# Renumbering the features of the expert gate/up matmuls so that the bf16 parts of the residual are written contiguously

## The reference, cut to what matters

```python
h = h + mixer(rmsnorm(h, norm_mix[i]))
h = h + hier_moe(rmsnorm(h, norm_ffn[i]), ...)

# hier_moe
grp_logits = xt @ w_grp + b_grp                      # 4 groups
exp_logits = einsum("td,gde->tge", xt, w_rt) + b_rt  # 4 experts in each
gate = ...   # top group, in it top 2 experts, softmax weights; (T, 16)
h = silu(einsum("td,edf->tef", xt, w_gate)) * einsum("td,edf->tef", xt, w_up)
y = einsum("tef,efd->td", h * gate[:, :, None], w_down)
```

## Time and profile before

| | |
|---|---|
| median of 3 runs | 1512.72 us |
| span of the profiled execution, first to last instruction | 1510.4 us |
| what lies around the span (median less span) | 2.3 us |
| TensorE busy | 1399.9 us (93%) |
| VectorE busy | 550.6 us (36%) |
| ScalarE busy | 438.2 us (29%) |
| GpSimd busy | 54.7 us (4%) |
| DMA | 480.62 MB, mean 318 GB/s |

### The profile page before, as it was taken

One profiled execution on the slowest core, in us unless ns is written; L12 is line 12 of the kernel. 1 busy time (PEld: TensorE's weight loads), 2 busy tenths in 40 slices (PEclk: granted clock), 3 DMA queues, 4 the chain that ended last, 5 costly groups with the idle time before them and its releaser, 6 DMA issues.

```text
span 1510.4 us, 22589 instructions
## 1 busy us (share of the span) xinstructions
PE 1399.9 (93%) x9100; PEld 775.0 (51%) x9100; DVE 550.6 (36%) x832; ACT 438.2 (29%) x585; POOL 54.7 (4%) x33
## 2 busy tenths in 40 slices
PE   6859999999999997999999997888999999999998
PEld 5634333433343345888888876665334333433433
DVE  3661221321222215656566664544212222122122
ACT  3860010110110004565656565552101100010000
POOL 0120000000000000101000001111000000000000
PEclk9969999999999999999999999998999999999999
DMA  9629899999999999554544443446989999999995
GB/s 337 262 92 386 329 421 421 423 421 423 421 422 421 422 414 332 187 176 158 168 165 167 167 140 112 150 160 279 359 359 422 422 422 422 421 422 421 422 422 236
DMA packets 94261, 480.62 MB, mean 318 GB/s; under 512 B 8451, under 2 KB 8549, under 8 KB 44805
## 3 DMA queue, kind: packets, MB, share of 16 engines
q1 hardware_dynamic: 93780, 477.07, 79.5%
q10 hardware_dynamic: 432, 2.88, 0.5%
HBM read 477.82 MB, written 2.10 MB: 318 GB/s over the span
## 4 chain that ended last, share of the span: by engine, by line
issue 52%; PE 37%; ACT 6%; DVE 3%; POOL 1%; DMA 1%; SPq 0%; POOLq 0%; ACTq 0%; DVEq 0%
PE ps L1303 15%; PE ps L1326 8%; PE ps L1174 4%; PE ps L1336 4%; PE ps L1259 3%; ACT parts L508 2%; ACT parts L515 1%; DVE ws L758 1%; ACT ws L492 1%; POOL head_rs L476 1%; DMA vec_rows<-in_q_norm 1%; ACT junk L505 1%; PE ps L1392 1%; DVE parts L778 0%; PE ps L1315 0%
## 5 line engine op out<-in xcount | busy, mean ns | idle before, releaser
L1303 PE MATMUL ps<-ring,xg 128*64 128x512 f32 x1968 | 432.0, 593 | 0.7 <-issue 0.7
L1174 PE MATMUL ps<-ws,xs 128*128 128x512 f32 x1632 | 393.5, 400 | 19.8 <-DVE ws L758 15.6
L1174 PEld LDWEIGHTS ps<-ws,xs 128*128 128x128 f32 x1632 | 310.0, 192 | 92.0 <-DVE ws L758 20.0
L1303 PEld LDWEIGHTS ps<-ring,xg 128*64 128x64 f32 x1968 | 142.8, 137 | 279.3 <-issue 279.3
L1326 PE MATMUL ps<-ring,hidT 128*64 128x512 f32 x1024 | 226.8, 595 | 21.9 <-ACT hidT L540 21.9
L913 DVE SCALAR_TENSOR_TENSOR hid<-ps,rs_slot,silu_g 64x512 f32<-64x512 f32 x32 | 24.1, 753 | 433.1 <-ACT silu_g L536 433.1
L536 ACT ACTIVATE silu_g<-ps,rs_slot 64x512 f32<-64x512 f32 x32 | 21.8, 682 | 516.8 <-PE ps L1303 516.8
L761 DVE SCALAR_TENSOR_TENSOR ws<-ring,vecs,ws 128x512 fp32r<-128x512 f32 x192 | 134.4, 747 | 92.4 <-ACT ws L495 92.4
L495 ACT ACTIVATE ws<-ring,vecs 128x512 fp32r<-128x512 f32 x192 | 127.4, 715 | 94.5 <-PE ps L1174 86.4
L1326 PEld LDWEIGHTS ps<-ring,hidT 128*64 128x64 f32 x1024 | 73.8, 137 | 151.2 <-issue 131.7
L1336 PE MATMUL ps<-y_rows,putT 128*128 128x512 f32 x256 | 123.4, 617 | 12.1 <-ACT y_rows L545 12.0
(11 more groups left out here) (153 smaller groups left out, 677.3 us busy)
## 6 DMA issues: line engine op xcount, KB each, us to landing
ring<-in_moe_w_down SPq DMA_DIRECT2D x128, 1024.0 KB, 15.3
ring<-in_moe_w_up SPq DMA_DIRECT2D x124, 1024.0 KB, 15.1
ring<-in_moe_w_gate SPq DMA_DIRECT2D x122, 1024.0 KB, 13.2
ring<-in_w_kv SPq DMA_DIRECT2D x32, 1024.0 KB, 5.4
ring<-in_w_q SPq DMA_DIRECT2D x16, 1024.0 KB, 5.0
ring<-in_w_o SPq DMA_DIRECT2D x16, 1024.0 KB, 5.0
extra<-in_moe_w_gate SPq DMA_DIRECT2D x6, 1024.0 KB, 7.8
ring<-in_pool_w SPq DMA_DIRECT2D x4, 1024.0 KB, 15.1
```

Of the source, the lines that this page charges most:

```text
L1174: last = mm(ps[:, bank + t, :], xs[:, px, k, cols], ws[:, b, pw, j, :], start=(first and j == 0 and n == 0), stop=(last_unit and j == 1 an ...
L1303: last = mm(ps[CAP * h:CAP * h + CAP, b, :], xg[:, b, k, :], both[h][:, j, :], start=(k == 0), stop=(k == KD - 1))
```

## The change

Features are numbered f = 512 q + 4 p + j instead of 16 p + k. Block q of the residual is now exactly the four tiles 4q to 4q+3, that is, columns 512 q to 512 q + 511 of `parts`; inside the block, feature 4 p + j is at column 128 j + p. The three parts are written in the order j, p, which is contiguous; `resid` is read in that order, with 4 floats (16 bytes) from one element to the next; `rest` keeps the new order and is written and read contiguously. The gate and up loads still give each partition four rows of 512 floats for each slot (8 KB), now rows 512 q + 4 p to 512 q + 4 p + 3; the four rows of neighbouring partitions follow each other in memory, where they were 32 KB apart. `ffn_gain` is loaded in pieces of four floats where it had sixteen in a row. The order of instructions, their number, their engines and the semaphores stay as they were.

```diff
-        w_gate_v = w_gate.rearrange("l e (p k) f -> l e p k f", k=KD)
-        w_up_v = w_up.rearrange("l e (p k) f -> l e p k f", k=KD)
+        w_gate_v = w_gate.rearrange("l e (q p j) f -> l e q p j f", q=NBLK, p=P)
+        w_up_v = w_up.rearrange("l e (q p j) f -> l e q p j f", q=NBLK, p=P)
...
         def in_tiles(s, t, c):
-            return parts[:, s, t, :].rearrange("q (k p) -> q p k", k=KD)[:, c * (BLK // KD):(c + 1) * (BLK // KD), :]
+            return parts[:, s, t, c * BLK:(c + 1) * BLK].rearrange("q (j p) -> q j p", j=4)
+        def rest_tiles(t):
+            return rest[:, t].rearrange("q (j p) -> q j p", j=4)
+        def resid_tiles(t, c):
+            return resid[:, t, c * BLK:(c + 1) * BLK].rearrange("q (p j) -> q j p", j=4)
...
-                    return (w_gate_v, w_up_v)[m % 2][l, e, :, 4 * (m // 2):4 * (m // 2) + 4, :]
+                    return (w_gate_v, w_up_v)[m % 2][l, e, m // 2]
...
-                sp.dma_start(ffn_gain[:, l, :], norm_ffn[l].rearrange("(p k) -> p k", k=KD)).then_inc(smalls_loaded, 16)
+                sp.dma_start(ffn_gain[:, l, :].rearrange("p (q j) -> p q j", j=4),
+                             norm_ffn[l].rearrange("(q p j) -> p q j", q=NBLK, j=4)).then_inc(smalls_loaded, 16)
...
 # first part, ScalarE
-                    nc.scalar.activation(in_tiles(0, t, c),
-                                         resid[:, t, c * BLK:(c + 1) * BLK].rearrange("q (p k) -> q p k", k=KD),
-                                         ACT.Copy).then_inc(hi_done, 1)
+                    nc.scalar.activation(in_tiles(0, t, c), resid_tiles(t, c), ACT.Copy).then_inc(hi_done, 1)
 # second part, ScalarE
-                nc.scalar.activation(in_tiles(1, t, c), rest[:, t].rearrange("q (p k) -> q p k", k=KD),
-                                     ACT.Copy).then_inc(mid_done[t], 1)
+                nc.scalar.activation(in_tiles(1, t, c), rest_tiles(t), ACT.Copy).then_inc(mid_done[t], 1)
 # rest, VectorE and GpSimd
-                nc.vector.tensor_tensor(rest[:, t].rearrange("q (p k) -> q p k", k=KD),
-                                        resid[:, t, c * BLK:(c + 1) * BLK].rearrange("q (p k) -> q p k", k=KD),
-                                        in_tiles(0, t, c), ALU.subtract).then_inc(rest_done[t], 1)
+                nc.vector.tensor_tensor(rest_tiles(t), resid_tiles(t, c), in_tiles(0, t, c),
+                                        ALU.subtract).then_inc(rest_done[t], 1)
 # third part, VectorE and GpSimd
-                nc.vector.tensor_tensor(in_tiles(2, 0, c), rest[:, 0].rearrange("q (p k) -> q p k", k=KD),
-                                        in_tiles(1, 0, c), ALU.subtract).then_inc(lo_done[0], 1)
+                nc.vector.tensor_tensor(in_tiles(2, 0, c), rest_tiles(0), in_tiles(1, 0, c),
+                                        ALU.subtract).then_inc(lo_done[0], 1)
```

More of the change, by code:

```diff
@@ L378, in again @@
                             for h, w in enumerate((w_gate_v, w_up_v)):
-                                sp.dma_start(four(2 * q + h), w[l, e, :, 4 * q:4 * q + 4, :]).then_inc(over[l]["loaded"], 16)
+                                sp.dma_start(four(2 * q + h), w[l, e, q]).then_inc(over[l]["loaded"], 16)
                             sp.dma_start(slot(8 + q), w_down_v[l, e, :, q, :]).then_inc(over[l]["loaded"], 16)
@@ L445, in left @@
                 pool.wait_ge(hi_done, 8 * l + 2 * c + 2)
-                nc.gpsimd.tensor_tensor(rest[:, 1].rearrange("q (p k) -> q p k", k=KD),
-                                        resid[:, 1, c * BLK:(c + 1) * BLK].rearrange("q (p k) -> q p k", k=KD),
-                                        in_tiles(0, 1, c), ALU.subtract).then_inc(rest_done[1], 1)
+                nc.gpsimd.tensor_tensor(rest_tiles(1), resid_tiles(1, c), in_tiles(0, 1, c),
+                                        ALU.subtract).then_inc(rest_done[1], 1)
             def third(l, c, t):
                 pool.wait_ge(mid_done[t], NBLK * l + c + 1)
-                nc.gpsimd.tensor_tensor(in_tiles(2, t, c), rest[:, t].rearrange("q (p k) -> q p k", k=KD),
-                                        in_tiles(1, t, c), ALU.subtract).then_inc(lo_done[t], 1)
+                nc.gpsimd.tensor_tensor(in_tiles(2, t, c), rest_tiles(t), in_tiles(1, t, c),
+                                        ALU.subtract).then_inc(lo_done[t], 1)
             def residual_parts(l):
```

## The result

The changed kernel takes 1464.88 us, the median of 4 runs (1464.04 to 1467.67), against 1512.62 us before: ratio 0.9688, 95% interval 0.9675 to 0.9702, 47.7 us less. Forecast were 1472 us, 40.5 us less, with a range of 1464 to 1487. Direction and mechanism came out as forecast; the size was 7 us short.

What follows compares the result with a forecast made beforehand. TensorE bounds the expert loops; between them it waits while ScalarE writes parts with stride. Layer 0 gives 18.0 us and layer 1 22.5, 40.5 off the 1510.4 span; with 2.3 around it 1472 us, range 1464 to 1487.

Steps and rivals of the forecast that it cites:

- Durations: Writers of parts: first 0.95 us, second 0.6, third 0.7 on VectorE or 1.3 on GpSimd; rest unchanged at 1.09 and 1.56.
- Layer 0 up to the logits: Start of layer 0 to the logits copy: with shorter part writes the copy starts at 75.75 instead of 91.45, 15.7 us.
- Layer 0, routing: Layer 0 behind the logits: VectorE's two stalls behind GpSimd's third parts shrink to some 1.4 us together, saving 2.3 us.
- Output projection: Layer 1, three blocks: shorter gap 2.8, clock held 1.6, two small gaps gone 1.4 us each block; 17.4 us in all.
- Layer 1, router: Layer 1, block 3 and routing: 2.85 us from ScalarE's first parts and 2.3 from shorter VectorE stalls; 5.1 us gain.
- Expert loops and loads: Expert loops of both layers: they start earlier, their own work and load rate unchanged; 0 us.
- rival 2: Expert loops: the new gate and up loads get slower, 1544 us at 380 GB/s; chance 0.04.
- Norm vector: Start of the kernel: its loads in smaller pieces are covered by some 10 us, nothing lost; without cover up to 6 us.
- Rival 1: First part on ScalarE: a strided read costs as much as the strided write, L508 stays at 2.4 us; 1494 us, chance 0.10.
- Rival 3: Routing and output projection: loops' start does not fully follow, through a second wait or slow clock; 1482 us, chance 0.13.
- The 2.3 us around the span: Time outside the profiled span, added to the forecast span of 1469.9 us to give 1472.2.
- behind 1.0 us the clock holds: Output projection: TensorE's 24 matmuls behind the shortened gap run at full clock, 5.73 instead of 7.34 us; 1.6 us a block.

Runs made afterwards that it cites:

- read_straight: The changed kernel with the residual read contiguously for the first part and the rest, features in another order; 1460.12 us, ratio 0.9659.
- pool_late: The kernel before, with GpSimd's two third parts of block 3 waiting until VectorE has made the first pick; 1514.91 us, ratio 1.0025.
- before_long: The kernel before with 46 instead of 24 small TensorE matmuls in each router while it waits for the routing; 1506.86 us, ratio 0.9965.
- first_old: The changed kernel with first part and rest strided as before, second and third part contiguous; 1491.7 us, ratio 0.9856.
- unit_first: The changed kernel with ScalarE's copy for unit 8c+10 moved ahead of the sums of squares and first part of block c; 1461.01 us, ratio 0.9670.
- loads_only: The changed kernel with the three parts written strided as before, only gate, up and norm vector loads new; 1512.16 us, ratio 0.9999 against the kernel before.
- later_old: The changed kernel with second and third part strided as before, first part and rest as changed; 1498.9 us, ratio 0.9915.

## Why the prediction was right, and where its sizes were off

1. *Durations.* Second part forecast 0.6 us (0.62 measured), third part 0.7 on VectorE (0.69) and 1.3 on GpSimd (1.18), first part 0.95 in a row of two (1.0). The row of L771, a strided read on another engine, was the right one to take the first part from: it gave 0.4 us for the read, and read_straight gives 0.49.
2. *Layer 0 up to the logits: 15.7 forecast, 14.8 measured.* The step that fell short is the rest of tile 0, which I left at 1.09 us. In the kernel before, GpSimd's rest ran at another time. Now both engines make their rest at once, and L777 takes 1.63 and 1.88 us in blocks 1 and 2, on the path, against 1.06 in block 0. That this is the same contention as in the routing is argued from the overlap in time; no run took it away.
3. *Layer 0, routing: 2.3 forecast, 5.4 measured.* The term for VectorE's stand behind GpSimd, 2.3, was 2.7, and pool_late shows the cause. The term that I did not have is the clock: VectorE's delay left TensorE idle for 3.2 us, and its next 106 matmuls ran slowly for it, 2.29 + 4.47 instead of 1.25 + 2.97 us. That is 2.5 us, and before_long gives 2.3 us for the same. I had the same effect in the sum in the output projection and left it out here, where the rows before show 4.47 us for the gather.
4. *Output projection: 17.4 forecast, 19.2 measured.* The 3.83 us left 0.96 as worked out (1.0), the clock held (1.6 us a block; first_old brings it back with 1.5, 2.4 and 2.8), the gaps of 0.89 and 0.48 us went. The 0.6 us a block that are over are the restart of the matmuls behind a gap, which costs some 0.3 us beside the gap, as unit_first shows, and two gaps a block went.
5. *Layer 1, router: 5.1 forecast, 5.6 and 6.8 measured.* The difference between the two profiles is the clock behind the router. Where the gap there closed, the ten matmuls and the gather took 1.25 + 2.97 instead of 1.69 + 3.98 us, 1.45 us that the forecast did not have; where it stayed, they took 1.56 + 4.10.
6. *Expert loops and loads: 0 forecast.* The loop of layer 1 is 473.5 us from its start to the end before and after. loads_only gives a ratio of 0.9999: rival 2 needed the loads to slow down, and they did not. (The 1968 matmuls of the prediction's reading are those of both loops, not of layer 1 alone; the wait of 0.7 us holds for both.)
7. *Norm vector: nothing, with 10 us of cover.* The cover is 39.4 - 28.3 = 11 us, and the second load went out 2.6 us later.
8. *Rival 1,* a read as dear as the strided write, is out by the row of L517. *Rival 3,* a late start of the loops, went the other way.
9. *The 2.3 us around the span* are 1.75 to 1.91 us in every run that has both numbers; the forecast was some 0.5 us too high by it.

The measured 47.7 us are thus the forecast's 40.5, less 0.9 for the contention of point 2, and more by some 3 in layer 0's routing, 2 in the output projection, 0.5 to 1.7 in layer 1's routing, and, where a run falls into the faster of the two groups, 1.5 us between the first loop and the output projection, where TensorE's matmuls behind the same waits ran at a higher clock. What puts a run into one group or the other stays open, and no run ties this last term to the change.

## What to carry to other kernels

Price every instruction's write by its stride before its operation: a bf16 write 256 bytes apart cost about four times a contiguous one on ScalarE and VectorE and twice on GpSimd, a strided read less than twice on each. When several waits lie one behind the other on the path, halves of a change undervalue it (13 and 20 us alone, 47 together), so work the whole schedule through. And where a wait of TensorE goes or comes, look at the duration of what it runs next, not only at the gap.

## What the runs showed of the hardware

- An instruction that writes 512 bf16 to each partition, 256 bytes apart, took 2.4 to 3.2 us on ScalarE, 2.5 to 2.8 on VectorE and on GpSimd, 5 ns or more an element; contiguous it took 0.62, 0.69 and 1.18 us. On VectorE and GpSimd one of the operands was read at that stride as well; such a read beside a contiguous write took 1.09 and 1.56 us (L771, L446), so the write is the greater part.
- A float read every 16 bytes cost ScalarE 0.49 us and VectorE 0.4 us more for 512 elements than a contiguous one.
- A VectorE instruction of 0.2 us stood for 2 us beside a running instruction of GpSimd.
- A gap of TensorE cost some 0.3 us beyond its own length, at the full clock on both sides (unit_first).
- Gaps of TensorE of the same length had different outcomes. Behind 2.37 us the 24 matmuls at 896.67 us of the changed kernel ran at full clock (5.76 us); the same 24 behind the same gap took 7.37 us in read_straight and 7.24 in before_long. Behind 2.48 us in later_old 48 took 12.80 us instead of 11.14, and behind 2.47 us, one block later, 12 took 3.04 us, the full clock again. The prediction's step "behind 1.0 us the clock holds" was right, but the row that it rested on, a gap of 2.37 us, could not have carried it either way.
